# A 512-token matmul in the output projection issued as two 256-token matmuls

## What is computed

```python
def short_conv_mixer(h, w_in, conv_w, w_out):
    b_gate, c_gate, v = jnp.split(h @ w_in, 3, axis=-1)
    u = c_gate * v
    y = causal_depthwise_conv(u, conv_w)        # width 3
    return (b_gate * y) @ w_out

x = x + short_conv_mixer(rmsnorm(x, mix_norm), conv_w_in, conv_w, conv_w_out)
a = relu(rmsnorm(x, mlp_norm) @ mlp_w1)
x = x + (a * a) @ mlp_w2
```

## Time and profile before

| | |
|---|---|
| median of 3 runs | 2105.51 us |
| span of the profiled execution, first to last instruction | 2104.1 us |
| TensorE matmul (PE) | 2094.3 us busy, 9220 instructions |
| weight loads (PEld) | 1732.8 us busy, 9220 instructions |
| VectorE (DVE) | 884.3 us busy |
| ScalarE (ACT) | 525.0 us busy |
| DMA | 210.35 MB, 100 GB/s over the span |

### The profile page before, as it was taken

One profiled execution on the slowest core, in us unless ns is written; L12 is line 12 of the kernel. 1 busy time (PEld: TensorE's weight loads), 2 busy tenths in 40 slices (PEclk: granted clock), 3 DMA queues, 4 the chain that ended last, 5 costly groups with the idle time before them and its releaser, 6 DMA issues.

```text
span 2104.1 us, 24666 instructions
## 1 busy us (share of the span) xinstructions
PE 2094.3 (100%) x9220; PEld 1732.8 (82%) x9220; DVE 884.3 (42%) x1337; ACT 525.0 (25%) x836; POOL 0.4 (0%) x5
## 2 busy tenths in 40 slices
PE   8999999999999999999999999999999999999999
PEld 7888888888888888888888888888888888888887
DVE  6344353443544454443334443334444333444332
ACT  6222222222233322222222222222222222222221
POOL 0000000000000000000000000000000000000000
PEclk9999999999999999999999999999999999999999
DMA  5322222222222222222222222222222222222223
GB/s 183 118 100 85 95 100 100 100 100 85 95 100 100 101 93 90 98 100 100 100 92 89 99 100 100 100 93 86 100 100 100 100 94 87 99 100 100 100 95 125
DMA packets 32731, 210.35 MB, mean 100 GB/s; under 512 B 3632, under 2 KB 3632, under 8 KB 8240
## 3 DMA queue, kind: packets, MB, share of 16 engines
q1 hardware_dynamic: 32544, 209.73, 27.7%
q10 hardware_dynamic: 144, 0.04, 0.0%
HBM read 205.56 MB, written 4.19 MB: 100 GB/s over the span
## 4 chain that ended last, share of the span: by engine, by line
PE 100%; DMA 0%; ACT 0%; DVE 0%; issue 0%; ACTq 0%
PE ps L398 99%; DMA cols<-in_cols 0%; PE ps L428 0%; PE ps L421 0%; PE ps L431 0%; PE ps L434 0%; ACT L170 0%; ACT h_hi L170 0%; DVE resid L301 0%; ACT w_hi L166 0%; ACTq L190 0%
## 5 line engine op out<-in xcount | busy, mean ns | idle before, releaser
L226 DVE TENSOR_TENSOR w_lo<-w_raw,w_hi 128x512 fp32r<-128x512 f32 x768 | 530.4, 693 | 1155.1 <-ACT w_hi L166 1142.1
L166 ACT ACTIVATE w_hi<-w_raw 128x512 fp32r<-128x512 f32 x768 | 484.9, 632 | 1529.2 <-PE ps L398 1526.1
L398 PE MATMUL ps<-h_hi,w_lo 128*128 128x512 f32 x1788 | 697.5, 390 | 0.1
L398 PE MATMUL ps<-h_lo,w_hi 128*128 128x512 f32 x1788 | 696.3, 389 | 0.0
L398 PE MATMUL ps<-h_hi,w_hi 128*128 128x512 f32 x1788 | 696.2, 389 | 0.0
L398 PE MATMUL ps<-z_lo,w_hi 128*128 128x512 f32 x1280 | 498.4, 389 | 0.0
L398 PE MATMUL ps<-z_hi,w_lo 128*128 128x512 f32 x1280 | 498.4, 389 | 0.0
L398 PE MATMUL ps<-z_hi,w_hi 128*128 128x512 f32 x1280 | 498.3, 389 | 0.0
L398 PEld LDWEIGHTS ps<-h_hi,w_lo 128*128 128x128 f32 x1788 | 335.9, 188 | 71.0 <-issue 1.6
L398 PEld LDWEIGHTS ps<-h_lo,w_hi 128*128 128x128 f32 x1788 | 335.9, 188 | 69.8 <-issue 0.5
L398 PEld LDWEIGHTS ps<-h_hi,w_hi 128*128 128x128 f32 x1788 | 335.7, 188 | 69.9
(11 more groups left out here) (30 smaller groups left out, 135.3 us busy)
## 6 DMA issues: line engine op xcount, KB each, us to landing
w_raw<-in_weights SPq DMA_DIRECT2D x191, 1024.0 KB, 4.8
out<-resid SPq DMA_DIRECT2D x16, 256.0 KB, 5.5
resid<-in_xt SPq DMA_DIRECT2D x3, 1024.0 KB, 12.6
resid<-in_xt SPq DMA_DIRECT2D x4, 256.0 KB, 5.5
w_raw<-in_weights SPq DMA_DIRECT2D x4, 256.0 KB, 6.2
cols<-in_cols ACTq DMA_DIRECT2D x1, 40.0 KB, 3.1
```

The lines of the kernel that those rows point to most:

```text
L166: nc.scalar.activation(w_hi[:, k % RING, :], w_raw[:, k // GRAN % NRAW, k % GRAN, :], ACT.Copy).then_inc(w_hi_ready, 1)
L226: nc.vector.tensor_tensor(w_lo[:, k % RING, :], w_raw[:, k // GRAN % NRAW, k % GRAN, :], w_hi[:, k % RING, :].bitcast(F32), ALU.subtract). ...
L398: mm = nc.tensor.matmul(ps[NT * parity + i][:], stationary, moving, start=(k == 0 and j == 0), stop=(k == KT - 1 and j == 2))
```

## The change

In the output projection, `half_products` stands in for `tile_products`. For each of the three products it issues two matmuls, over tokens 0 to 255 and 256 to 511, into the two halves of the same bank, with the same stationary tile. The start flag is set for the first half of the first product alone. The waits, the count-up of `w_used` after a slice's last matmul, and all work of the other engines stay as they are; the other 44 blocks go on with `tile_products`.

```diff
--- before.py
+++ after.py
@@ -399,11 +399,23 @@
                                           stop=(k == KT - 1 and j == 2))
                 return mm
 
-            def products(b, k, parity, act):
+            def half_products(k, i, parity, act):
+
+                whi, wlo = (w[:, k % RING, P * i:P * (i + 1)] for w in (w_hi, w_lo))
+                hi, lo = (a[:, k, :] for a in act)
+                for j, (stationary, moving) in enumerate(((wlo, hi), (whi, lo), (whi, hi))):
+                    for half in range(2):
+                        cut = slice(S // 2 * half, S // 2 * (half + 1))
+                        mm = nc.tensor.matmul(ps[NT * parity + i][:, cut], stationary, moving[:, cut],
+                                              start=(k == 0 and j == 0 and half == 0), stop=(k == KT - 1 and j == 2),
+                                              skip_group_check=True)
+                return mm
+
+            def products(b, k, parity, act, tile=tile_products):
 
                 pe.wait_ge(w_lo_ready, KT * b + (k + 1))
                 for i in range(NT):
-                    mm = tile_products(k, i, parity, act)
+                    mm = tile(k, i, parity, act)
                 mm.then_inc(w_used, 1)
 
             def banks_free(b):
@@ -452,7 +464,7 @@
                     for k in range(KT):
                         if sub == 0:
                             pe.wait_ge(z_ready, k + 1)
-                        products(2 * two + sub, k, sub, Z)
+                        products(2 * two + sub, k, sub, Z, half_products)
 
 
             banks_free(MLP0)
```

## The result

The changed kernel takes 2116.82 us (median of 3 runs, 2116.42 to 2117.19) against 2105.51 before. The ratio is 1.0053, 95% interval 1.0033 to 1.0073: slower by 11.3 us, 6.9 to 15.4.

The account below looks back on a forecast made before the run. TensorE's matmul pace was taken to bound the kernel: 2105.5 + 10.2 (halves at 120.0 ns) + 1.0 (loop edges) = 2116.7 us. The range was 2103 to 2143 us, the forecast's own 2111 to 2129.

Parts of the forecast that it names:

- What bounds the kernel: Whole kernel: TensorE's own pace alone counts, matmuls being busy 2094.3 of 2104.1 us; the other engines keep ahead.
- The pace of a half, 120.0 ns: Output projection: a 256-column matmul takes 106.7 ns of stream plus 13.3 ns excess; 1536 of them cost +10.2 us.
- a toll per matmul: Output projection: the 13.3 ns above the stream is paid once per weight load; forecast 2111 to 2129 us, chance 0.53.
- The lower bound, 108 to 110 ns: Output projection: least pace of a 256-column matmul, set by how soon one weight load can follow another.
- The restart's single distance: At 1056 us, after TensorE ran dry, two weight loads started 0.11 us apart, read as a load's turnaround.
- The 0.16 us read off the start: At the kernel's start (6.53 to 6.69 us): distance between two weight loads, taken to be at the lower clock.
- The loop edges, +1.0 us: Output projection's loop, three edges: shorter queued matmuls run out before new instructions come, +1.0 us, bounds nothing and 3 us.
- Excess per column: Rival, output projection: the excess goes by the column, a half takes 113.3 ns, total 2105.5 to 2108 us; chance 0.20.
- One path for 640 columns (136.0): Rival, output projection: load and stream share one path, a half takes 136.0 ns, +34.8 us, 2140 us; chance 0.11.
- A load's full record as the pace (188 or 227): Rival, output projection: each matmul waits a load's whole record or cycle, +114.7 or +174.1 us; chance 0.10.
- Faster by way of the turnaround alone: Rival, output projection: short matmuls run at the load's 108 ns without excess, -8.2 us, 2097.3 us; chance 0.04.
- The clock: Rival, output projection: TensorE's clock falls to its lower level, a half takes 213.8 ns, +154 us, 2260 us; chance 0.02.

## Why the prediction was right

**What bounds the kernel**: right. The other engines' busy time did not move, and TensorE has no new wait in the stage.

**The pace of a half, 120.0 ns**: right to the digit; the stage took 184.31 us for 184.3. The step that led there was a choice between a toll per matmul and a toll per column, given as 0.53 and 0.20. The run with 384 columns (0.174 us a step) settles it for float32r with full loads. The reason that I gave for the choice, a load that takes its columns from a stream at full rate, was not borne out: with half the load's columns the pace at 512 was 230.0, not lower, and the excess was 16.7 ns there and at most 8.6 at 192 columns. So the number rests on three widths (512, 384, 256), and its cause stays open.

**The lower bound, 108 to 110 ns**: a little low. The restart's single distance was 0.11; the floor in a long row is 111.7. That it is the load's turnaround is right: with half as wide a load the pace at 192 columns fell to 88.6. The 0.16 us read off the start as the same distance at the lower clock is not the floor there: that is 0.214 at a granted clock of 0.50. (At the start the profile gives a granted clock of 1.00; the prediction took the lower level from the pace of 427.5 ns.)

**The loop edges, +1.0 us**: wrong. Nothing stands idle at the output projection's edges, in, round or out, and the microsecond forecast at L461's end isn't there. A gap of 2.0 us did open at this loop's head once the blocks ahead of it were split too. The gap that did grow in the profile, 0.07 to 0.67 us at 1066 us, is in the unchanged kernel as well when profiled again. The sum came within 0.1 us of the median because the difference of the medians happens to be 11.3, with an interval of 6.9 to 15.4; the traces alone say 10.2.

**The rivals.** Excess per column: no for float32r with full loads; for the most part yes for bfloat16 in 4-byte steps; open for float32r with half loads. One path for 640 columns (136.0): no, 120.0. A load's full record as the pace (188 or 227): no, records overlap. Faster by way of the turnaround alone: no. The clock: 1.00 in this kernel, so no; in the kernel that is split nearly everywhere it was 0.63 and 0.50 behind two of the 2 to 3 us gaps (mean 0.998).

## What to carry to other kernels

In a kernel that TensorE bounds, count the matmuls as well as their columns: take the pace from the chain (time over count), subtract the columns at the granted clock, and ask at a second width whether what is left is paid once per instruction (float32r here) or by the column (bfloat16 in 4-byte steps). Look in the trace for a restart after an idle stretch, where two loads follow each other unhindered: it hints at the least distance of two matmuls (0.11 us, and 111.7 ns in a row), and a split is cheap only while the columns stay above it (256 cost 6% more than 512 here, 128 cost twice as much). Where types are mixed on TensorE, group them, and read the pace behind each change.

## What the runs showed of the hardware

- A float32r matmul with its load of 128 columns took its own columns plus 13.3 ns (226.7, 173.5 and 120.0 ns at 512, 384 and 256 columns) and at least 111.7 ns (192 and 128 columns). At a granted clock of 0.50 that floor was 214 ns.
- In bfloat16 the excess was some 2.5 ns without gaps between elements (216 and 109 ns at 512 and 256), and 5.5 to 6.2% of the columns' time with steps of 4 bytes (225.0 and 113.3).
- A change from bfloat16 to float32r and back costs 20 ns on the paces of three when every third matmul is float32r (678.3 against 658.3).
- Loading 64 columns in place of 128 shortened the load's record from 0.19 to 0.13 us and made a 512-column matmul no faster (230.0 ns), but a 192-column one faster (88.6 against 111.7). So the floor is the load's. What the 13.3 ns are stays open: they are neither the load's in proportion to its width nor the same at any width.
- Behind two of three idle stretches of 2.0 to 2.6 us the granted clock was 0.63 and 0.50 (562.3 to 565 and 1675.9 to 1679 us in the kernel split nearly everywhere); behind one of 0.6 us (the kernel before, again) and within the long rows it was 1.00.
